# Two transformer blocks on one core: the kernel's beginning is reordered (operand halves read from PSUM, small vectors loaded by another queue, first row scale one step later)

## What is computed

```
h = rms_norm(r, g_mix)        # y = x * rsqrt(mean(x*x) + eps);  h = y * g
z = h @ w_in                  # 2048 x 11264
q, k, v, c_b, c_c, c_x, g_a, g_c = split(z)
...                           # attention, a short convolution, gates
r = r + merged @ w_o          # then an MLP, a gated side input,
...                           # then the second block: convolution of 31 taps, SwiGLU
```

## Time and profile before

| | us |
|---|---|
| median of 3 runs | 2796.67 |
| lowest and highest | 2795.59, 2797.86 |
| span of the profiled execution | 2794.7 |
| PE busy in it | 2585.7 (93%) |
| DVE, ACT, POOL busy | 1904.8, 1273.6, 524.6 |
| DMA over the span | 465.19 MB, 166 GB/s |

### The profile page before, as it was taken

How to read it: one execution, slowest core, us unless ns; L and a number is a source line. 1 busy time by engine, 2 the same in 40 slices (tenths; PEclk the granted TensorE clock), 3 DMA queues, 4 the chain that set the end, 5 groups by cost and what they waited for, 6 DMA issues and landing times.

```text
span 2794.7 us, 44956 instructions
## 1 busy us (share of the span) xinstructions
PE 2585.7 (93%) x15005; PEld 2281.7 (82%) x15005; DVE 1904.8 (68%) x2097; ACT 1273.6 (46%) x1583; POOL 524.6 (19%) x307
## 2 busy tenths in 40 slices
PE   6999899999999999999999955557799999999998
PEld 5888788888888888888888955546678888888887
DVE  5568875677765666656677799996586646665665
ACT  4455545555544444444455422205544444444444
POOL 3024410002000000000113965744320000000002
PEclk8999999999999999999999988878999999999999
DMA  4555456555555555656555522302445555555553
GB/s 156 180 181 173 136 173 188 196 190 184 175 187 188 189 191 182 195 188 188 181 183 177 166 79 86 120 31 83 158 148 188 188 184 188 187 192 189 187 183 120
DMA packets 464573, 465.19 MB, mean 166 GB/s; under 512 B 14411, under 2 KB 461381, under 8 KB 464453
## 3 DMA queue, kind: packets, MB, share of 16 engines
q1 hardware_dynamic: 463984, 463.92, 52.0%
q10 hardware_dynamic: 516, 0.38, 0.1%
HBM read 462.15 MB, written 2.10 MB: 166 GB/s over the span
## 4 chain that ended last, share of the span: by engine, by line
PE 79%; DVE 10%; issue 6%; ACT 1%; DMA 1%; POOL 1%; DVEq 1%; ACTq 0%; POOLq 0%
PE gp L355 51%; PE gp L357 26%; DVE work L1359 3%; DVE sq L1359 2%; DVE wlo L1044 1%; POOL work L1639 1%; DVE A L1096 1%; DVE A L1105 1%; DMA work<-in_conv_w_dw 1%; ACT whi L652 1%; DVEq L1358 0%; DVE work L1362 0%; PE gp L351 0%; PE gp L353 0%; PE gp L352 0%
## 5 line engine op out<-in xcount | busy, mean ns | idle before, releaser
L1044 DVE TENSOR_TENSOR wlo<-stage,whi 128x1024 fp32r<-128x1024 f32 x812 | 1008.8, 1258 | 692.3 <-ACT whi L652 687.2
L355 PE MATMUL gp<-A,whi 128*128 128x512 f32 x3968 | 1401.1, 396 | 29.0 <-DVE A L1096 15.4
L652 ACT ACTIVATE whi<-stage 128x1024 fp32r<-128x1024 f32 x876 | 914.7, 1056 | 1082.9 <-PE gp L357 883.4
L357 PE MATMUL gp<-A,wlo 128*128 128x256 f32 x3968 | 1118.9, 282 | 0.0
L355 PEld LDWEIGHTS gp<-A,whi 128*128 128x128 f32 x3968 | 751.0, 189 | 203.2 <-issue 22.4
L355 PE MATMUL gp<-B,whi 128*128 128x512 f32 x2496 | 874.0, 395 | 14.9 <-DVE B L1396 13.3
L357 PEld LDWEIGHTS gp<-A,wlo 128*128 128x128 f32 x3968 | 754.3, 190 | 0.4
L357 PE MATMUL gp<-B,wlo 128*128 128x256 f32 x2496 | 700.2, 281 | 0.0
L355 PEld LDWEIGHTS gp<-B,whi 128*128 128x128 f32 x2496 | 468.3, 188 | 123.4 <-issue 15.7
L357 PEld LDWEIGHTS gp<-B,wlo 128*128 128x128 f32 x2496 | 472.4, 189 | 0.1
L1606 POOL TENSOR_TENSOR wlo<-stage,whi 128x1024 fp32r<-128x1024 f32 x64 | 200.7, 3159 | 84.6 <-ACT whi L652 84.3
(11 more groups left out here) (234 smaller groups left out, 1428.4 us busy)
## 6 DMA issues: line engine op xcount, KB each, us to landing
stage<-in_w_in SPq DMA_DIRECT2D x160, 512.0 KB, 4.1
stage<-in_w_up SPq DMA_DIRECT2D x128, 512.0 KB, 3.8
stage<-in_w_down SPq DMA_DIRECT2D x128, 512.0 KB, 4.0
stage<-in_ffn_w_gate SPq DMA_DIRECT2D x88, 512.0 KB, 4.4
stage<-in_ffn_w_up SPq DMA_DIRECT2D x88, 512.0 KB, 4.4
stage<-in_ffn_w_down SPq DMA_DIRECT2D x88, 512.0 KB, 3.3
stage<-in_conv_w_in SPq DMA_DIRECT2D x64, 512.0 KB, 3.7
stage<-in_w_o SPq DMA_DIRECT2D x32, 512.0 KB, 4.3
```

The source lines that it names most:

```text
L355: nc.tensor.matmul(bank.rearrange("p (a t) -> p a t", a=2), hi, both_parts(M, kt), start=first, stop=False)
L357: done = nc.tensor.matmul(bank[:, T:2 * T], lo, M[:, kt, 0:T], start=False, stop=last)
L652: nc.scalar.activation(whi[:, slot, :], stage[:, slot, :], ACT.Copy).then_inc(hi_ready, 1)
L1044: nc.vector.tensor_tensor(wlo[:, slot, :], stage[:, slot, :], whi[:, slot, :].bitcast(F32), ALU.subtract).then_inc(lo_ready, 1)
```

## The change

It edits the beginning only. The 18 vector DMAs are issued by SP, after the input and weight units 0 to 3 and ahead of weight unit 4. The gain's transpose comes first on PE. Each input chunk is turned into a home of its own in PSUM (`x_home`: `xp` banks 2 and 3, `gp` banks 2 and 3, `xp` banks 0 and 1, `xp` banks 2 and 3 again), chunks 2 and 3 only after units 0 and 1 of the first step. ACT makes the high parts and DVE the low parts straight from there; the copy to `r` comes later. ACT and DVE take a weight unit ahead of the chunk, not behind it. `column_sums(0)` and the row scale move from qkv step 0 to step 1; what step 0 made is scaled then.

```diff
+        def x_home(c):
+            return [xp[:, 2:4, :], gp[:, 2:4, :], xp[:, 0:2, :], xp[:, 2:4, :]][c].rearrange("p a (b t) -> p (a b) t", b=2)
...
             for c in range(4):
                 sp.dma_start(xt[:, :, 512 * c:512 * c + 512], xv[:, :, 512 * c:512 * c + 512]).then_inc(x_loaded[c], 16)
                 load(c, c, win[:, 4 * c:4 * c + 4, 0:HPW], first=True)
+            order = [("g_mix", 0, 0), ("g_mlp", 0, 16), ("g_ple", 0, 32), ("conv_b_in_2", 0, 48), ("conv_b_dw_2", 0, 80),
...
+            for name, half, row in order:
+                n = io[name].shape[1] // P
+                sp.dma_start([V1, V2][half][row:row + n, :], io[name].rearrange("o (k p) -> (o k) p", p=P)).then_inc(v_loaded, 16)
+            for t in range(3):
+                sp.dma_start(V2[82 + 8 * t:90 + 8 * t, :],
+                             io["w_conv"][0, t:t + 1, :].rearrange("o (k p) -> (o k) p", p=P)).then_inc(v_loaded, 16)
+            sp.dma_start(taps_raw, io["conv_w_dw_2"].rearrange("o t d -> (o t) d")).then_inc(v_loaded, 16)
             panel(4, 0, win, 0, KT, HPW)
...
-                    if u == 0:
+                    if u == 0 and not (isinstance(hp, int) and hp == 0):
                         pe.wait_ge(evacuated, XSLOTS + hp - 1)
...
             pe.wait_ge(consts, 4)
-            for c in range(4):
-                j = c % 2
+            pe.wait_ge(gain_loaded, 16)
+            nc.tensor.transpose(xp[:, 1, 0:KT], first_gain, ident[0:KT, 0:KT]).then_inc(vec_turned, 1)
+
+            def turn_x(c):
                 pe.wait_ge(x_loaded[c], 16)
-                if c >= 2:
-                    pe.wait_ge(evacuated, c - 1)
+                if c == 2:
+                    pe.wait_ge(vec_ready, 1)
+                if c == 3:
+                    pe.wait_ge(h1_ready, 4)
+                    pe.wait_ge(evacuated, 1)
...
-                        done = nc.tensor.transpose(gp[:, 2 * j + kk // 2, o:o + P], xt[:, t, kt * P:kt * P + P], ident[:])
+                        done = nc.tensor.transpose(x_home(c)[:, kk, t * P:t * P + P], xt[:, t, kt * P:kt * P + P], ident[:])
                 done.then_inc(x_turned, 1)
...
+            turn_x(0)
+            turn_x(1)
...
-            body("qkv", 0, A, h1, {4: [lambda: column_sums(0)]})
+            body("qkv", 0, A, h1, {0: [lambda: turn_x(2)], 1: [lambda: turn_x(3)]})
 
             pe.wait_ge(v_loaded, 16 * 18)
...
-            with pe.Fori(1, 5) as it:
+            body("qkv", 1, A, h1, {4: [lambda: column_sums(0)]})
+            with pe.Fori(2, 5) as it:
                 body("qkv", it, A, h1)
...
-            for c in range(4):
+            def hi_of_x(c):
                 act.wait_ge(x_turned, c + 1)
-                j = c % 2
-                nc.scalar.activation(r[:, 4 * c:4 * c + 4, :].rearrange("p (a b) t -> p a (b t)", a=2),
-                                     gp[:, 2 * j:2 * j + 2, :], ACT.Copy).then_inc(evacuated, 1)
...
+                for kk in range(4):
+                    nc.scalar.activation(A[:, 4 * c + kk, 0:T], x_home(c)[:, kk, :], ACT.Copy,
+                                         scale=col("g_mix", 4 * c + kk)).then_inc(x_hi, 1)
+
+            def copy_x(c):
+                act.wait_ge(h1_ready, 4 * c + 4)
+                nc.scalar.activation(r[:, 4 * c:4 * c + 4, :], x_home(c), ACT.Copy).then_inc(evacuated, 1)
+
+            take_hi(0, 0, 0)
+            hi_of_x(0)
+            take_hi(1, 0, 1)
+            hi_of_x(1)
+            copy_x(0)
+            take_hi(2, 0, 2)
+            hi_of_x(2)
+            copy_x(1)
+            take_hi(3, 0, 3)
+            hi_of_x(3)
+            copy_x(2)
+            copy_x(3)
...
-            body("qkv", 0, root_first(0, none), {u: vectors[3 * u:3 * u + 3] for u in range(6)})
+            body("qkv", 0, none)
...
+            body("qkv", 1, root_first(0, none))
...
             for c in range(4):
-                for kt in range(4 * c, 4 * c + 4):
-                    dve.wait_ge(x_hi, kt + 1)
-                    nc.vector.scalar_tensor_tensor(A[:, kt, TM:TM + T], r[:, kt, :], col("g_mix", kt),
+                take_lo(c, c)
+                for kk in range(4):
+                    kt = 4 * c + kk
+                    dve.wait_ge(x_hi, 4 * c + 2 * (kk // 2) + 2)
+                    nc.vector.scalar_tensor_tensor(A[:, kt, TM:TM + T], x_home(c)[:, kk, :], col("g_mix", kt),
                                                    A[:, kt, 0:T].bitcast(F32), ALU.mult, ALU.subtract).then_inc(h1_ready, 1)
-                take_lo(c, c)
...
+            def first_rstd():
+                variance(0, 0, RMS_EPS)
+                four = qkv_flat[:, 0:4, :]
+                nc.vector.tensor_tensor(four, four, by_rstd(4), ALU.mult).then_inc(qkv_ready, 2)
...
+            body("qkv", 0, lambda hp, it, j: add_up(hp, j, qkv_at(it, j)))
+            body("qkv", 1, normed_into(qkv_at, qkv_ready, first_rstd))
```

More of the change, by code:

```diff
@@ L278, in _ @@
                 load(c, c, win[:, 4 * c:4 * c + 4, 0:HPW], first=True)
+            order = [("g_mix", 0, 0), ("g_mlp", 0, 16), ("g_ple", 0, 32), ("conv_b_in_2", 0, 48), ("conv_b_dw_2", 0, 80),
+                     ("conv_ln_g_2", 0, 96), ("conv_ln_b_2", 0, 112), ("conv_b_out_2", 1, 0), ("norm_mix_pre_2", 1, 16),
+                     ("norm_mix_post_2", 1, 32), ("norm_ffn_pre_2", 1, 48), ("norm_ffn_post_2", 1, 64), ("g_q", 1, 80),
+                     ("g_k", 1, 81)]
+            for name, half, row in order:
[5 more added lines that the diff above has]
+            sp.dma_start(taps_raw, io["conv_w_dw_2"].rearrange("o t d -> (o t) d")).then_inc(v_loaded, 16)
             panel(4, 0, win, 0, KT, HPW)
@@ L708, in _ @@
             act.dma_start(first_gain, io["g_mix"].rearrange("o (k p) -> (o k) p", p=P)).then_inc(gain_loaded, 16)
[L709 to L722, removed]
             act.wait_ge(vec_turned, 1)
@@ L793, in _ @@
             nc.scalar.activation(taps2[:].rearrange("p k t -> p (k t)"), xp[:, 3, 0:KT * TAPS2], ACT.Copy).then_inc(vec_ready, 1)
-            with act.Fori(1, 5) as it:
+            body("qkv", 1, root_first(0, none))
+            with act.Fori(2, 5) as it:
                 body("qkv", it, none)
@@ L1113, in tail @@
                     add_up(hp, j, d)
-                    if first and j == 0 and isinstance(it, int) and it == 0:
+                    if first and j == 0:
                         first()
@@ L1176, in beside, with qkv_at @@
                         7: [output(i - 1)] if i else []}
[L1178 to L1181, removed]
+            def first_rstd():
+                variance(0, 0, RMS_EPS)
+                four = qkv_flat[:, 0:4, :]
+                nc.vector.tensor_tensor(four, four, by_rstd(4), ALU.mult).then_inc(qkv_ready, 2)
+            def qkv_at(it, j):
+                return qkv_flat[:, ds(4 * it + 2 * j, 2), :]
+            qkv_tail = normed_into(qkv_at, qkv_ready)
+            body("qkv", 0, lambda hp, it, j: add_up(hp, j, qkv_at(it, j)))
+            body("qkv", 1, normed_into(qkv_at, qkv_ready, first_rstd))
+            with dve.Fori(2, 5) as it:
                 body("qkv", it, qkv_tail)
```

7 lines of the change are left out of this document (removed).

## The result

| | us |
|---|---|
| changed kernel, median of 4 runs | 2769.46 (2767.16 to 2775.42) |
| kernel before, median of 4 runs beside it | 2797.27 (2795.59 to 2797.98) |
| ratio, with its 95% interval | 0.9905 (0.9892 to 0.9918) |
| forecast | 2777.0 (2772 to 2786) |

The change gains 27.8 us; 19.5 were forecast, and the time lies under the whole range. The profiled execution is the slowest of the four: it took 2775.42 us, its span is 2773.6, 21.1 less than before. So the traces speak for 21.1 of the 27.8 us (23.7 in the second profile, also the slowest of its four runs); what makes the faster executions 4 to 6 us faster still stays open.

What follows compares the result with a forecast made beforehand. It took TensorE's matmuls as the bound, with 12.11 us idle at the start for the taps' DMA. Unit 8 at 46.4 instead of 65.9 gains 19.5: 2794.7 - 19.5 = 2775.2, plus 2.0 for the median: 2777; range 2772 to 2786.

Steps and rivals of the forecast that it cites:

- The row scale's cover: qkv step 1: row scale and a weight unit take 7.4 us, hidden behind 8.4 us of TensorE work.
- Low parts beside POOL: VectorE at the start: low parts read from PSUM take 0.47 us each even while POOL works; bounds 0.42 and 1.32.
- the rivals: Start: unit 4 not held back, 2773.5 (0.12); small transfers slower, 2785 to 2788 (0.12), 2791 to 2802 (0.05), 2837 (0.04).
- the 17 small transfers: SP's queue: expected to keep pace, last issue at 16 us; rival of 0.5 to 0.7 us each, 2785 to 2788, chance 0.12.
- the 4 to 6 that were named as the sign: TensorE ahead of unit 4: a wait of 4 to 6 us at 27 to 33 us, ended by a weight load.
- The term T: Landing of weight unit 4 behind the taps on SP's queue: 16 + 0.6 + 10.9 + 1.7 = 29.2 us; bounds 24.4 and 35.1.
- The restart: TensorE at unit 4, after idling some 5 us: the lower clock costs 1.7 us more.
- the prediction's own mark: Unit 8, first of qkv step 1: 65.9 us to compare with before, 46.4 forecast, a gain of 19.5 us.
- The sum: From unit 8 to the end: every start about 19 us earlier, so 2794.7 - 19.5 = 2775.2 us in the profile.

Runs made afterwards that it cites:

- second profile: The changed kernel run once more, unaltered, beside the kernel before: 2771.58 us, ratio 0.99.
- pad12: Kernel before with twelve tiny writes that compute nothing added at the head of VectorE's stream: 2787.64 us, ratio 0.9972.
- rstd_only: Kernel before with only the column sums and row scale moved from qkv step 0 to step 1: 2786.3 us, ratio 0.9956.
- dve_unroll: Kernel before with qkv step 1 written out ahead of the loop on VectorE alone: 2786.38 us, ratio 0.9961.
- loop_out: Kernel before with VectorE's three-round loop in the 31-tap convolution written out: 2784.28 us, ratio 0.996.
- before_split: Kernel before with the 31-row taps DMA issued as two of 16 and 15 rows, still from ACT: 2782.98 us, ratio 0.9947.
- split: Changed kernel with the 31-row taps DMA issued as two of 16 and 15 rows: 2761.31 us, ratio 0.9869 to the kernel before.
- split_whole_x: Changed kernel with taps in two transfers but without operand halves from PSUM (input copied to SBUF first): 2771.5 us, ratio 0.9913 to the kernel before.
- halves_only: Kernel before with only the operand halves from PSUM in their new order; vectors on ACT, row scale in step 0: 2795.09 us, ratio 0.999.
- vec_rstd: Changed kernel without operand halves from PSUM; vectors on SP and row scale in step 1 kept: 2772.52 us, ratio 0.9914 to the kernel before.

## Why the prediction was right and wrong

**Right.** The wait for `in_conv_w_dw` is gone and one for a weight unit stands ahead of unit 4, caused as forecast: unit 4 queued behind the 31 rows on one engine. The first unit starts at 10.36 (forecast 10.2). The row scale's cover holds. Low parts beside POOL cost 0.41 us (0.47 forecast). None of the rivals happened: the 17 small transfers kept their pace (the taps issued at 15.1, 16 forecast). But the idle time ahead of unit 4 is 10.04 us, twice the 4 to 6 that were named as the sign. TensorE was through with units 0 to 3 at 24.5, not at 27.0, since the chunks turned behind units 0 and 1 take 1.03 us at the full clock, not 1.97, and unit 4 starts at 34.56, not at 32.3.

**The term T.** Unit 4 landed at 31.6, not 29.2, inside the bounds. The packets of the taps run from 16.0 (16.6 forecast) to 29.5 us. They are 0.3 apart while nothing else moves, and up to 0.6 while weight units load beside them: 13.5 us for 31, where 10.9 were taken (31 x 0.35, the 0.35 from a stretch with a share of other traffic). From their end to the landing it takes 2.1 us, against 1.7.

**The restart.** From unit 4 to unit 8 it takes 34.56 to 49.64, 15.1 us. Four units of 2.79 and 1.4 of transposes leave 2.5 for the lower clock, where 1.7 was taken; the transposes' 1.4 were put at 1.2. With T's 2.4 these (0.8 and 0.2) make the 3.2 us by which unit 8 (49.64) is later than forecast (46.4), less 0.1 that high and low part took less. So 65.9 - 49.6 = 16.3 us by the prediction's own mark, and 15 to 16.5 later on. Too much was expected of the start, by 3 to 4 us.

**What it did not have.** No term and no rival spoke of the 9.6 us in the convolution. The sum was carried from 65.9 us to the end by the sentence that every start from there on is 19 us earlier. That is the step that failed. It took for granted that instructions which stay the same take the same time, but the edit of step 1 moves all of VectorE's later instructions by eleven. pad12 shows that the place alone does it; rstd_only and dve_unroll fit (9.7 and 9.6 us). The waits of the kernel before had the sign: `DVE work L1350 <- issue: 11.0, 2, 5.5` is a wait on nothing at the head of an engine's loop, on the path of TensorE, far from the change. The two errors have opposite signs; without the 9.6 us the time would have been near 2779, inside the range. That would have been luck in part: the start gave 3 to 4 us too little, 2 to 3 are lost behind 1903, and the 4 to 6 us by which the median lies under the profiled execution are explained by nothing here.

**Credit by part.** The prediction spread its gain over an earlier first unit and an earlier landing of the vectors. In the runs the move of the vectors gives 14.2 of the start's 15.5 us alone, the halves 1.3 by themselves (2795.09) and 1 to 3 on top, as their 6 us of head start mostly lengthen the wait for unit 4. The prediction's own sum could have told so: its T contains no term of the halves.

**Where 2 to 3 us go again.** Behind an idle time of 13.26 us at the layer norm TensorE restarts at the lower clock in both kernels, at 1918.63 and at 1894.12. Ten us around the restart, before and then after:

```profile
1918.00:1928.00 10.00, 9.37 (x45) 8.22 (x46) 6.87 (x11) 9.81 (x19) 0.00 (x0) 0.81 0.01 2
```
```profile
1893.00:1903.00 10.00, 8.88 (x35) 7.66 (x36) 7.36 (x12) 9.81 (x19) 0.00 (x0) 0.64 0.01 2
```

The second stretch begins 0.5 us earlier against the restart; from 1893.49 its clock is 0.67, still under 0.81. The clock comes back 6.0 us behind the restart after, 3.2 before. Instruction against instruction that costs 1.3 us; another 1.6 are lost bit by bit from there to 2007, at the full clock. Other runs lose here as well: dve_unroll, pad12 and loop_out 2.2 to 2.9 us by the end, before_split 2.6 and split 2.4, though in these two the clock comes back after 3.1 and 2.9; rstd_only loses 0.5, split_whole_x and halves_only nothing. So it goes neither with this change nor with the faster convolution, and the clock is only a part of it; the cause stays open.

## What to carry to other kernels

Before a DMA is put into a queue that feeds the critical stream, see in the packets on how many engines it runs: the 31 rows here went one at a time, and the weight units issued behind them landed only when that engine was through; splitting them into 16 and 15 gave 14 us in the old kernel and 8 to 10 in the new one. When two limits end close together, an edit that lifts one shows nothing until the other goes, so the worth of an edit must be asked for again after each one. And where code is written out or added on an engine, ask also what lies behind it: a wait "<-issue" at the head of a long loop can come or go by a dozen instructions.

## What the runs showed of the hardware

- Where a loop's instructions lie decided whether its two jumps cost 5.5 us each. VectorE's loop of some 357 instructions lost them at the 792nd instruction, not at the 803rd or 804th, and not when written out. Which places are bad, and why there the instruction packets come 13 times instead of 2 to 5, was not settled: only these places were tried.
- A queue whose one engine is behind holds up the issues too. In the changed kernel SP's issue of unit 6 took 8.3 us (16.37 to 24.7) and unit 7 followed only then, though from 20 to 25 us the sixteen engines were busy for 7.5% of the time; unit 7 landed 10.9 us after its issue. In split no issue of a unit up to 27 us took over 0.51 us. By the Trainium skill, DMA: Bandwidth & Descriptors, "Why a DMA increments its semaphore by 16 and not by 1", a transfer takes the largest number of engines up to 16 that divides its outer dimension. The trace agrees at 31 rows (one packet of 8 KB at a time); with 16 and 15 the waits of 10.04 and 12.11 us fell to 1.93 and 0.50.
- Four low parts took 1.66 us from PSUM and 5.28 from SBUF on a VectorE beside a busy POOL (the second in vec_rstd). The Trainium skill, SBUF — State Buffer, "Who interferes with whom", says that VectorE's second SBUF port is the one it shares with GpSimd. The trace agrees that the form with two SBUF operands is the one that pays, and shows how much.
